# Second attention: the value products of a pair in one group, in the next pair's second step

## The reference, cut to what matters

```python
# forgetting attention, heads 0 to 7
s = einsum('bqhd,bkhd->bhqk', qb, k) * scale + F[t] - F[s];  causal mask
p = softmax(s);  y = einsum('bhqk,bkhd->bqhd', p, v)
# indexer sparse attention, heads 0 to 7 of its own q, k, v
sc = einsum('bqhd,bkd->bqhk', qib, k_idx) * idx_scale
iscore = einsum('bqhk,bqh->bqk', relu(sc), w);  _, sel = top_k(iscore, 128)
logits over the selected keys + T5 bias;  p = softmax(logits);  y = p @ v
```

## Time and profile before

| | |
|---|---|
| median of 3 runs | 1367.6 us (1365.65 to 1367.89) |
| the profiled execution | 1367.89 us |
| its span in the profile | 1366.1 us |
| TensorE matmul busy | 1349.1 us, 99% |
| VectorE busy | 828.0 us, 61% |
| ScalarE busy | 519.4 us, 38% |
| GpSimd busy | 572.9 us, 42% |
| GpSimd's subtractions L539 | 222, 569.9 us |
| TensorE's granted clock | 0.994 of full speed |

### The profile page before, as it was taken

The page is one execution under the profiler, slowest core; times in us unless marked ns, Lnnn a source line. Parts: engine busy times, 40 slices in busy tenths (PEclk is TensorE's granted clock), DMA queues, the critical chain, the costliest instruction groups (busy, mean ns, idle before and its releaser), DMA issues.

```text
span 1366.1 us, 18059 instructions
## 1 busy us (share of the span) xinstructions
PE 1349.1 (99%) x6370; PEld 1097.0 (80%) x6374; DVE 828.0 (61%) x1089; ACT 519.4 (38%) x822; POOL 572.9 (42%) x230
## 2 busy tenths in 40 slices
PE   9999999999999999999999999999999999999998
PEld 7788878888888888877777777888878888888886
DVE  5565577594774857868978864433555243352465
ACT  6333224322312314245366665323345223142233
POOL 4333434463563735434222223444434535354361
PEclk9999999999999999999999999999999999999999
DMA  8222235655675655423513223333423324223231
GB/s 255 80 80 80 87 115 170 171 172 171 175 202 150 175 159 149 122 68 87 93 47 94 78 78 93 93 94 89 147 62 109 117 77 123 77 92 120 79 94 62
DMA packets 212807, 156.72 MB, mean 115 GB/s; under 512 B 8932, under 2 KB 193632, under 8 KB 212616
## 3 DMA queue, kind: packets, MB, share of 16 engines
q1 hardware_dynamic: 212280, 155.40, 39.9%
q10 hardware_dynamic: 464, 0.48, 0.1%
HBM read 153.73 MB, written 4.74 MB: 116 GB/s over the span
## 4 chain that ended last, share of the span: by engine, by line
PE 49%; DVE 4%; issue 1%; ACT 1%; DVEq 0%; ACTq 0%
PE ps L578 28%; PE ps L1100 11%; PE ps L1049 3%; PE ps L965 1%; PE ps L952 1%; DVE work L2226 1%; PE ps L1130 1%; DVE top L2224 1%; PE ps L938 1%; PE ps L939 1%; DVE work L2244 1%; DVE work L2241 0%; PE ps L942 0%; PE ps L899 0%; PE ps L903 0%
## 5 line engine op out<-in xcount | busy, mean ns | idle before, releaser
L539 POOL TENSOR_TENSOR w_lo<-raw,w_hi 128x1024 fp32r<-128x1024 f32 x222 | 569.9, 2575 | 761.6 <-ACT w_hi L1185 744.7
L578 PE MATMUL ps<-u_hi,w_hi 128*128 128x512 f32 x944 | 379.7, 402 | 4.4 <-DVEq L2293 3.3
L578 PE MATMUL ps<-u_hi,w_lo 128*128 128x512 f32 x944 | 369.2, 391 | 0.0
L578 PE MATMUL ps<-u_lo,w_hi 128*128 128x512 f32 x944 | 369.0, 391 | 0.0
L1185 ACT ACTIVATE w_hi<-raw 128x1024 fp32r<-128x1024 f32 x222 | 232.8, 1054 | 266.7 <-PE ps L1100 91.0
L578 PEld LDWEIGHTS ps<-u_hi,w_hi 128*128 128x128 f32 x944 | 178.8, 189 | 41.5 <-issue 4.9
L578 PEld LDWEIGHTS ps<-u_hi,w_lo 128*128 128x128 f32 x944 | 177.9, 188 | 37.9
L578 PEld LDWEIGHTS ps<-u_lo,w_hi 128*128 128x128 f32 x944 | 178.2, 189 | 35.3 <-issue 1.0
L578 PE MATMUL ps<-y_hi,w_hi 128*128 128x512 f32 x320 | 125.2, 391 | 0.1
L578 PE MATMUL ps<-y_hi,w_lo 128*128 128x512 f32 x320 | 124.5, 389 | 0.0
L578 PE MATMUL ps<-y_lo,w_hi 128*128 128x512 f32 x320 | 124.5, 389 | 0.0
(11 more groups left out here) (305 smaller groups left out, 1919.1 us busy)
## 6 DMA issues: line engine op xcount, KB each, us to landing
raw<-w_in SPq DMA_DIRECT2D x69, 512.0 KB, 3.8
raw<-w_mlp SPq DMA_DIRECT2D x64, 512.0 KB, 3.9
adaw<-w_ada SPq DMA_DIRECT2D x32, 768.0 KB, 4.6
raw<-w_up SPq DMA_DIRECT2D x32, 512.0 KB, 6.0
raw<-w_down SPq DMA_DIRECT2D x32, 512.0 KB, 6.0
raw<-w_out SPq DMA_DIRECT2D x16, 512.0 KB, 4.6
bias_rows<-bias_rows SPq DMA_DIRECT2D x4, 635.0 KB
xtok<-x SPq DMA_DIRECT2D x4, 512.0 KB, 7.8
```

The costliest lines, as they stand in the source:

```text
L539: pool.tensor_tensor(w_lo[:, s, :], raw[:, s, :], w_hi[:, s, :], ALU.subtract).then_inc(lo_ready[s], 1)
L578: last = pe.matmul(ps[0:cols, bank, :], w[:, s, c], r[:, k, :], start=(k == ks[0] and w is w_hi and r is r_hi), stop=(k == ks[-1] and w is ...
```

## The change

On TensorE, all four value products of a pair stand in one group, in step 1 of the next pair (20 matmuls); the group in step 5 is gone. After the last pair, the group behind the loop has all four as well. The copy of the first turned even tile moves on VectorE from step 0 (behind the divisions) to step 1 (behind its logits). On ScalarE, the exp of step 1 moves ahead of the evacuation of the first odd tile.

```diff
             for p in range(2 * NQ):
                 for n in range(8):
                     if n == 1 and p > 0:
-                        pv(p - 1, 2)
-                        pv(p - 1, 3)
-                    if n == 5:
-                        pv(p, 0)
-                        pv(p, 1)
+                        for i in range(NT):
+                            pv(p - 1, i)
                     t_step(p, n)
...
             pieces.pop(0)()
-            pv(2 * NQ - 1, 2)
-            pv(2 * NQ - 1, 3)
+            for i in range(NT):
+                pv(2 * NQ - 1, i)
...
                 coming_exp(p, 0)
+                coming_exp(p, 1)
                 turned_odd(p, 0)
-                coming_exp(p, 1)
...
                     if n % 2 == 0:
                         coming_weights(p, n)
-                        if n < 6:
+                        if n in (2, 4):
                             turned_even(p, n // 2)
                     coming_logits(p, n)
+                    if n == 1:
+                        turned_even(p, 0)
```

## The result

| | before | after |
|---|---|---|
| median | 1366.16 us (20 runs, 1364.11 to 1367.89) | 1368.47 us (20 runs, 1366.70 to 1370.02) |
| the profiled execution | 1367.89 us | 1368.93 us |
| its span | 1366.1 us | 1367.1 us |

The ratio is 1.0014, with a 95% interval of 1.0008 to 1.0020. The changed kernel is slower by 1.9 us by the ratio (1366.16 x 0.0014) and by 2.3 by the medians. The forecast had 2.9, on a median before of 1367.6; with 20 runs that median is 1366.16. By the ratio the change stays inside the 0.2% that the prediction calls no change. It is resolved all the same, since the interval leaves out 1.

The account below looks back on a forecast made before the run. TensorE bounds the kernel, busy 1349.1 of 1366.1 us. Terms 1.86 + 1.23 - 0.15 + 0 - 0.04 = +2.9 us took the profiled 1367.89 to 1370.8, or 1370.5 against the median; range 1365.8 to 1373.0.

Parts of the forecast that it names:

- Term 1: TensorE's value groups: step 5 loses 0.96 us, step 1 of the next pair gains 0.65, so -0.31 in each place.
- Term 2: Step 6, pairs 0 to 6: TensorE waits 0.72 us for GpSimd's w_lo; only 0.24 gained, net +0.41 us per pair.
- Term 3: VectorE's later copy of the first turned tile: +0.21 us each in pairs 1 to 3, 0 in pairs 5 to 7.
- Pair 4: Low parts come earlier, but step 2's turning waits some 0.2 us for the copy: -0.15 us, between -0.27 and +0.41.
- Pair 0: No value group; step 2's wait for the later copy falls into the existing low-parts stall: 0, at most +0.35 us.
- Term 4: Pair 7, the end: 0.69 us gained up to GpSimd's subtraction, 0.65 given to the longer last group: -0.04 us.
- The bounds: Range of the forecast case with the bounds of its terms: 1369.5 to 1372.7 us.
- The first rival: Step 6 does not wait because GpSimd's part is ready in time: -1.7 us, 1365.9 us; chance 0.27.
- The second: The drain alone counts: the copy hides and pairs 1 to 4 lose part of their stalls: -2.5 us, 1365.1; chance 0.08.
- The third: GpSimd shuts out VectorE's divisions in pairs 1 to 3 too: +1.9 us on top, 1372.4 us; chance 0.07.

Follow-up runs that it names:

- copy_back: Changed kernel with the first even tile's copy and ScalarE's two instructions back at their old places; 1368.59 us, ratio 1.0010 to before.
- cast_at_keys: Changed kernel with the copy at its old place and slot 1's cast behind the keys' high parts (pair 7's cast unmoved); 1365.10 us, ratio 0.9985 to before.
- early_cast: Changed kernel with ScalarE's cast for slot 1 ahead of the exp that step 3 calls; 1368.02 us, ratio 1.0007 to before.

## Why the prediction was right

- **Term 1, the group.** One group of 20 takes 2.48 us; 2.47 was worked out. The saving of 0.31 us that it leaves if nothing waits showed itself once w_lo came early: 0.27 to 0.32 per stretch.
- **Term 2, the piece of step 6.** Foretold: a wait of 0.72 us for w_lo, net +0.41 per pair. The load comes 0.72 us behind the mask's load in pair 2, as booked; by the view's own count six of the seven waits are 0.61 to 0.66. The copy_back kernel, which has this term alone, pays +0.42 in stretches 1 to 3 and 0.38 and 0.43 in 6 and 7. That this chain and not something else is the cause is shown by moving its start: with the cast at the keys the wait and the cost are both gone. The slack of 0.24 held: from the end of the low parts to the load took 744.58 - 739.05 = 5.53 before and 744.12 - 738.83 = 5.29 after (738.14 + 0.69 = 738.83).
- **Term 2 in pair 5** (stretch 5, which holds step 6 of pair 4) was the largest error of the sum: +0.41 booked, +0.10 measured. I let all seven pairs wait alike, though I had booked pair 4 to run otherwise. After the change the first scores of pair 4 are no longer held by the low parts. These end 0.41 us ahead of them, against 0.11 before (779.48 - 778.68 - 0.69). Timeline after:

```profile
778.78 0.69 DVE L2297 TENSOR_TENSOR k_both<-ps,k_both 64x512 fp32r<-64x512 f32 x1
779.63 0.49 PE L952 MATMUL ps<-small,prob_evens 128*128 128x128 f32 x3
...
779.88 0.31 PE L938 MATMUL ps<-k_both,q_up 128*128 128x128 f32 x1
...
784.76 0.19 PEld L578 LDWEIGHTS ps<-u_hi,w_hi 128*128 128x128 f32 x1 [0.33 <-POOL w_lo L539]
```

The chain to w_lo starts at the low parts, so it is 0.30 us ahead of TensorE there, and the wait is 0.33 where the others have 0.62. In copy_back, where pair 4 is held as before, stretch 5 pays the +0.40.
- **Term 3, the copy.** +0.21 in pairs 1 to 3 and nothing in 5 to 7 were booked. Alone it costs 0.20 and 0.01 on the mean; on top of the group it costs 0.24 in stretches 1 to 3. Together these stretches measured +0.69, +0.62 and +0.66 against +0.62 each.
- **Pair 4.** -0.15 booked, -0.05 measured. The turning of step 2 waits for the copy, 0.16 us at 774.99, where about 0.2 was foretold.
- **Pair 0.** 0 booked, 0.00 measured ahead of its first scores in step 4. The turning of step 2 waits 0.58 us for the copy there (693.60), and the stall at the first scores takes it in, as foretold: they stand 698.31 - 698.05 = 0.26 us behind the turning, where 1.00 was before.
- **Term 4, the end.** -0.04 booked, -0.20 measured. I halved a row of two subtractions, 5.17 us. The two are not equal: the longest of this part takes 2.83, so the other has 2.34. After the change the load came at 843.91 without a wait, behind a subtraction that began at 841.46, so the first of the two had at most 2.39. With 842.53 instead of 842.78 for its end the slack of before was 0.94 and the term -0.29. The 0.09 us from there to the measured -0.20 were not traced.
- **The sum.** The terms gave +2.9, the stretches +2.58, the medians +2.3 and the ratio +1.9. Against the stretches the two mis-sized terms were 0.47 too high, stretches 1 to 4 ran 0.21 over and stretches 6 and 7 0.06 under: 2.9 - 0.47 + 0.21 - 0.06 = 2.58. So part of the errors cancelled, but no term had the wrong sign. The medians (2.3) and the ratio (1.9) see the same effect through runs whose clock moves them by over 3 us, so they can't confirm the first decimal. As a time, 1370.5 lies 2.0 above the measured 1368.47: 1.4 of it is the median before, taken from three runs, and 0.6 the sum.
- **The bounds.** 1369.5 to 1372.7 is not what the bounds of the terms add up to. With them the sum reaches from about 1365.4 (no wait in six pairs, no cost of the copy, pair 4 at -0.27) to 1373.1 (no slack, the copy's 0.29, pair 4 at +0.41, pair 0 at +0.35). No reading rests on them.

The first rival, that step 6 doesn't wait, falls with the seven waits. The second, the drain alone, falls with it: its -2.5 us are what cast_at_keys nearly reaches (-2.03 in the attention). The third didn't come by the change: the divisions of 128x256 that it names keep their 0.62 us in pairs 1 to 3 after (709.67, 730.01, 750.30), and those of 128x512 take 7.1 us in all before and after. But four experiments ran into it at other instructions.

## What to carry to other kernels

Before booking the time that a removal frees on the bounding engine, follow that engine to the next thing it has to wait for and read the slack there: of 0.96 us freed, 0.24 could be used. Then start that other chain earlier in the same edit, at a place where its engines don't meet. When you move VectorE's or GpSimd's work, look at which of the two starts first at every place where they come near, and read small effects from the period of a repeated stage inside the profile before asking the medians.

## What the runs showed of the hardware that was not expected

- **Who starts first decides, within tenths of a microsecond.** Near GpSimd's subtraction of 2.4 to 2.5 us, two divisions of 128x256 took 2.74 us instead of 0.62, two of 128x512 1.85 instead of 0.88, and the mask of 128x512 2.28 instead of 0.43. In pair 7 of early_cast each of two divisions met a subtraction of its own: 4.21. Divisions that started 0.33 ahead of GpSimd kept their 0.62, those 0.14 ahead took 2.74; the row holds two, and the second of them starts behind GpSimd. The late ones end 0.15 to 0.30 us behind GpSimd, and 0.67 to 0.69 in pairs 0 to 4 of early_cast, where a second division was still to do. The Trainium skill, SBUF — State Buffer, section "SBUF: two separate sides", says that GpSimd and a VectorE instruction in a 2-port mode, or with two inputs in SBUF, share a port pair, and that whichever starts first holds it to its end. The rows of the divisions and the masks agree; no view names an instruction's mode.
- **Not all of VectorE's work is hit.** In the changed kernel, under the subtraction that runs from 741.68 to 744.07, a MAX8 over 128x512 took 0.69 and a MATCH_REPLACE8 0.68 us:

```profile
742.36 0.69 DVE L2221 MAX8 top<-work 128x8 f32<-128x512 f32 x1
743.09 0.09 DVE L2223 MATCH_VALUE_LOAD work<-top,work 128x8 f32 x1
743.16 0.68 DVE L2223 MATCH_REPLACE8 work<-top,work 128x512 f32<-128x512 f32 x1
```

The same pair a little later (744.09 and 744.89), with GpSimd idle, took 0.69 and 0.68 too. The keys' low parts, which read PSUM, took 0.68 and 0.69 under GpSimd in cast_at_keys (735.03 and 735.75). So of this kernel's work the selection rounds and the low parts may lie under GpSimd, and divisions and masks may not. Why they differ was not tried.
